# A two-block sequence model on one core: output products of eight finished tiles set between the steps of the last scan

## The reference, cut to what matters

```python
branches = [(ya, a_z), (yb, b_z), (yc, c_z), (yd, d_z), (ym, m_z)]
mixed = jnp.concatenate([y.astype(x.dtype) * jax.nn.silu(z) for y, z in branches], axis=-1)
return x + mixed @ w_out
```

```python
def step(state, inp):
    r_t, w_t, k_t, v_t, kk_t, a_t = inp
    sa = jnp.einsum("bhvk,bhk->bhv", state, -kk_t)
    state = (state * w_t[:, :, None, :] + sa[..., None] * (kk_t * a_t)[:, :, None, :]
             + v_t[..., None] * k_t[:, :, None, :])
    return state, jnp.einsum("bhvk,bhk->bhv", state, r_t)
...
y = rms_norm(y.swapaxes(0, 1), ln_g.reshape(GROUP_HEADS, HEAD_DIM))
y = y + jnp.sum(rh * kh * r_k, axis=-1, keepdims=True) * vh
```

## Time and profile before

| what | us |
|---|---|
| median of three runs | 1772.87 |
| the profiled execution | 1763.42 |
| its span, first to last instruction | 1761.7 |
| pairs, 1565 to 1592 | 27.0 |
| doubling, 1592 to 1643.4 | 51.4 |
| `WT`, `MTt` v and `U`, to 1655.87 | 12.5 |
| scan with all outputs, 1655.87 to 1695.20 | 39.3 |
| output products under the y chain, to 1708.07 | 12.9 |
| turning, gating and splitting y, to 1711.44 | 3.4 |
| the other output products, to 1758.50 | 47.1 |
| last add and store | 3.2 |

### The profile page before, as it was taken

How to read it: one execution, slowest core, us unless ns; L and a number is a source line. 1 busy time by engine, 2 the same in 40 slices (tenths; PEclk the granted TensorE clock), 3 DMA queues, 4 the chain that set the end, 5 groups by cost and what they waited for, 6 DMA issues and landing times. The chain is left out here.

```text
span 1761.7 us, 23121 instructions
## 1 busy us (share of the span) xinstructions
PE 1608.7 (91%) x9729; PEld 1341.3 (76%) x9729; DVE 720.7 (41%) x1479; ACT 519.5 (29%) x841; POOL 593.6 (34%) x247
## 2 busy tenths in 40 slices
PE   6998999999989988989897998999999877959899
PEld 6896876999979765866675997897887643649889
DVE  4031430331163635977665125312301555586331
ACT  2443224331123123243343112342221235211211
POOL 5333420433333263534642333332442360500213
PEclk8999999999999988999998999999999786578869
DMA  4313220225223220320111422242222000000102
GB/s 147 90 57 94 72 72 1 75 94 179 96 72 97 77 79 24 96 72 24 49 48 32 173 73 84 96 128 78 91 95 72 1 0 1 0 30 1 64 26 98
DMA packets 116721, 121.58 MB, mean 69 GB/s; under 512 B 14607, under 2 KB 110841, under 8 KB 116362
## 3 DMA queue, kind: packets, MB, share of 16 engines
q1 hardware_dynamic: 113072, 114.16, 20.6%
q10 hardware_dynamic: 3546, 5.94, 0.9%
HBM read 113.80 MB, written 6.29 MB: 68 GB/s over the span
## 5 line engine op out<-in xcount | busy, mean ns | idle before, releaser
L175 POOL TENSOR_TENSOR w_low<-w_ring,w_high 128x2048 fp32r<-128x2048 f32 (+2 forms) x95 | 422.5, 4448 | 896.9 <-ACT w_high L166 896.8
L191 PE MATMUL ps<-w_high,xT_high 128*128 128x256 f32 (+1 forms) x1056 | 305.9, 290 | 9.9 <-issue 6.9
L191 PE MATMUL ps<-w_high,xT_low 128*128 128x256 f32 (+1 forms) x1056 | 300.9, 285 | 0.0
L191 PE MATMUL ps<-w_low,xT_high 128*128 128x256 f32 (+1 forms) x1056 | 300.9, 285 | 0.0
L166 ACT ACTIVATE w_high<-w_ring 128x2048 fp32r<-128x2048 f32 (+2 forms) x95 | 174.1, 1833 | 362.4 <-PE ps L191 349.7
L191 PE MATMUL ps<-xT_high,w_high 128*128 128x512 f32 (+3 forms) x624 | 255.4, 409 | 8.7 <-DVE mix_a L724 7.7
L191 PE MATMUL ps<-xT_low,w_high 128*128 128x512 f32 (+3 forms) x624 | 250.8, 402 | 0.0
L191 PE MATMUL ps<-xT_high,w_low 128*128 128x512 f32 (+3 forms) x624 | 249.4, 400 | 0.0
L191 PEld LDWEIGHTS ps<-w_high,xT_high 128*128 128x128 f32 x1056 | 204.8, 194 | 15.2 <-issue 14.9
L191 PEld LDWEIGHTS ps<-w_low,xT_high 128*128 128x128 f32 x1056 | 204.8, 194 | 1.3 <-issue 1.2
L191 PEld LDWEIGHTS ps<-w_high,xT_low 128*128 128x128 f32 x1056 | 204.2, 193 | 0.0
(11 more groups left out here) (500 smaller groups left out, 2416.3 us busy)
## 6 DMA issues: line engine op xcount, KB each, us to landing
w_ring<-in_gla_w_in_dram SPq DMA_DIRECT2D x24, 1024.0 KB, 5.4
w_ring<-in_dsa_w_in_dram SPq DMA_DIRECT2D x19, 1024.0 KB, 5.2
w_ring<-in_w_in_dram SPq DMA_DIRECT2D x18, 1024.0 KB, 5.1
w_ring<-in_gla_w_out_dram SPq DMA_DIRECT2D x8, 1024.0 KB, 5.2
w_ring<-in_ple_gate_w_dram SPq DMA_DIRECT2D x8, 1024.0 KB, 5.0
w_ring<-in_dsa_w_out_dram SPq DMA_DIRECT2D x8, 1024.0 KB, 5.0
w_ring<-in_w_out_dram SPq DMA_DIRECT2D x8, 640.0 KB, 4.3
x_scratch<-x SPq DMA_DIRECT2D x4, 1024.0 KB, 6.9
```

The lines of the kernel that those rows point to most:

```text
L175: self.nc.gpsimd.tensor_tensor(self.w_low[:, i % RING, 0:k, 0:cols], self.w_ring[:, n % RING, 0:k, 0:cols], self.w_high[:, i % RING, 0:k, ...
L191: return self.nc.tensor.matmul(out, lhs, rhs, start=first, stop=last, skip_group_check=not check)
```

## The change

- `w_out` is cut the other way: four chunks of 256 columns by the eight finished tiles, and a fifth of 1024 columns by the two own tiles. `slot` lets a ring slot hold the fifth chunk's shape. Each chunk is loaded by one or two DMAs.
- The products of the finished tiles are 16 **units** (`early_out`), one for a chunk and a token tile, 24 split products of 256 columns each, in two banks of PSUM that take turns. VectorE adds each unit to `x_back` (`early_added`). Units 0 to 7 stand in the eight steps of the scan, between the k products and the wait for `sa`; 8 and 9 behind the scan; 10 to 15 behind the last outputs.
- The outputs stand behind the S products instead of ahead of them, two for a step from the second on; the last two behind unit 9. Their four heads share a bank now, and the scaling of y reads them without a permutation.
- The own tiles' products are eight groups (4 token tiles by 2 halves of 512 columns) of 6 split products, at the very end.
- ScalarE makes the first chunk's high half and the high halves of the finished tiles at the start of the block. GpSimd makes that chunk's low half at once, then waits for the four `TiT_init`, then makes `mix_low`.
- To free memory for that, `RKT` gets its own tensor, `Cm` takes the place of `bt`, and `Ti` and `TiT` take the slots of the second chunk.
- The bonus products are made ahead of the scan; VectorE waits for `x_back` there; SP loads a third chunk before `x_back`.

On TensorE, one step of the scan before (the third): `WT` with the state, then k with v (`rwkv_tok`), then two outputs, each with `RKT` (here a part of `branch_room`), `RBT` and the state, then S (`sa,rwkv_tok`).

The diff, cut to its core (`add_sources`, `add_rows` and the removed `project` are told above):

```diff
-        g.add_chunks(t["w_out_2"][0], 0, D, most=MIX_TILES // 2 * P)
+        for a in range(0, D, CHUNK):
+            g.add_rows(t["w_out_2"][0], [(0, OWN_TILES[0]), (OWN_TILES[-1] + 1, MIX_TILES)], a, a + CHUNK)
+        g.add_rows(t["w_out_2"][0], [(OWN_TILES[0], OWN_TILES[-1] + 1)], 0, D)
...
+        RKT = new("RKT", [P, NT, GH, P])
...
-        Ti, RKT = rooms[first_slot], rooms[1 - first_slot]
-        Cm, TiT = rooms[2 + first_slot][:, 0:2], rooms[3 - first_slot]
+        Ti, TiT = rooms[1 - first_slot], rooms[3 - first_slot]
+        Cm = bt[:].rearrange("p a (h t) -> p a h t", h=GH)
+        bonus_v = MTt[:].rearrange("p j h t -> p (j h t)")[:, 0:NT * GW].rearrange("p (j d) -> p j d", j=NT)
...
+                def early_out(u):
+
+                    c, j = early_units[u]
+                    if j == 0:
+                        chunk[0] = g.chunk(pe, w_out + c)
+                    if u == 0:
+                        pe.wait_ge(sem["mix_low"], past["mix_low"] + len(early))
+                    if u < 2:
+                        pe.wait_ge(sem["U_copied"], past["U_copied"] + NT)
+                    else:
+                        pe.wait_ge(sem["early_added"], past["early_added"] + u - 1)
+                    for i, k in enumerate(early_tiles):
+                        ins = g.split_product(ps[:, early_bank(u), 0:CHUNK], columns(s.mix_parts, k, slice(j * P, (j + 1) * P)), columns(chunk[0], i),
+                                              i == 0, i == len(early_tiles) - 1)
+                    ins.then_inc(sem["early_ready"], add("early_ready", 1))
+                    if j == NT - 1:
+                        g.release("early_ready")
...
-
-                    for n in range(2 * (c - 2), 2 * (c - 1)):
-                        if n >= 0:
-                            output(*outputs[n])
-                    pe.wait_ge(sem["sa_ready"], past["sa_ready"] + 2 * c + 2)
+                    early_out(first_early[c])
+                    pe.wait_ge(sem["sa_ready"], past["sa_ready"] + c + 1)
                     for cols, out in place:
                         ins = g.product(out, tok[toks, 0, j, cols], sa[toks, j, cols], False, True, check=False)
                     ins.then_inc(sem["S_ready"], add("S_ready", 1))
-                for n in range(2 * (NCH - 2), len(outputs)):
+                    for n in range(2 * (c - 1), 2 * c):
+                        if n >= 0:
+                            output(*outputs[n])
+                early_out(NCH)
+                early_out(NCH + 1)
+                pe.wait_ge(sem["early_added"], past["early_added"] + NCH + 1)
+                for n in range(2 * (NCH - 1), len(outputs)):
                     output(*outputs[n])
...
+                for u in range(NCH + 2, len(early_units)):
+                    early_out(u)
                 pe.wait_ge(sem["y_final"], past["y_final"] + NT)
                 to_gated(g, pe, y, [4, 5])
+                w = g.chunk(pe, w_out + D // CHUNK)
+                pe.wait_ge(sem["state_new"], past["state_new"] + PAIRS * NCH)
+                pe.wait_ge(sem["early_added"], past["early_added"] + len(early_units))
+                pe.wait_ge(sem["y_gated"], past["y_gated"] + len(OWN))
                 pe.wait_ge(sem["own_low"], past["own_low"] + len(OWN))
-                project(0, 1, OWN, True)
-                for n in range(1, D // CHUNK):
-                    for c in range(2):
-                        project(n, c, halves[c], True)
+                for u, (n, j) in enumerate(own_units):
+                    for i, k in enumerate(OWN):
+                        ins = g.split_product(ps[:, own_bank(u), :], columns(s.mix_parts, k, slice(j * P, (j + 1) * P)), columns(w, i, slice(n * COLS, (n + 1) * COLS)),
+                                              i == 0, i == len(OWN) - 1)
+                    ins.then_inc(sem["own_ready"], add("own_ready", 1))
+                g.release("own_ready")
...
             def _(act):
+                g.split_high(act, w_out + 1)
+                for tiles in early:
+                    nc.scalar.activation(s.mix_parts[0][:, tiles, :], s.mixT[:, tiles, :], ACT.Copy).then_inc(sem["mix_high"], add("mix_high", 1))
...
-                for j in range(NT):
+                g.split_high(act, w_out + 3)
+
+                def y_squares(j):
                     act.wait_ge(sem["y_ready"], past["y_ready"] + j - j % 2 + 2)
-                    sq = RBT[:, j, 0:2, :].rearrange("p h t -> p (h t)").rearrange("p (i b d) -> p b i d", b=2, d=HD)
-                    nc.scalar.activation(sq, y_in(j), ACT.Square).then_inc(sem["y_sq"], add("y_sq", 1))
+                    nc.scalar.activation(RBT[:, j, 0:2, :].rearrange("p h t -> p (h t)"), y_in(j), ACT.Square).then_inc(sem["y_sq"], add("y_sq", 1))
+
+                y_squares(0)
+                y_squares(1)
+                g.split_high(act, w_out + 4)
+                y_squares(2)
+                y_squares(3)
                 act.wait_ge(sem["y_mean_sq"], past["y_mean_sq"] + 1)
                 nc.scalar.activation(ss[:], ss[:], ACT.Sqrt).then_inc(sem["y_root"], add("y_root", 1))
-                g.split_high(act, w_out + 2)
+                g.split_high(act, len(g.chunks))
...
             def _(pool):
-                pool.wait_ge(sem["X_ready"], past["X_ready"] + doubled)
                 g.split_low(pool, w_out + 1)
+                pool.wait_ge(sem["TiT_init"], past["TiT_init"] + NT)
                 for i, tiles in enumerate(early):
                     pool.wait_ge(sem["mix_high"], past["mix_high"] + i + 1)
                     nc.gpsimd.tensor_tensor(s.mix_parts[1][:, tiles, :], s.mixT[:, tiles, :], s.mix_parts[0][:, tiles, :].bitcast(F32), ALU.subtract).then_inc(sem["mix_low"], add("mix_low", 1))
...
+                dve.wait_ge(sem["x_back"], past["x_back"] + 16)
+
+                def early_added(u):
+
+                    c, j = early_units[u]
+                    cols = slice(c * CHUNK, (c + 1) * CHUNK)
+                    dve.wait_ge(sem["early_ready"], past["early_ready"] + u + 1)
+                    nc.vector.tensor_tensor(x_back[:, j, cols], x_back[:, j, cols], ps[:, early_bank(u), 0:CHUNK], ALU.add).then_inc(sem["early_added"], add("early_added", 1))
...
+                    early_added(first_early[c])
...
             def _(sp):
+                g.load_chunks(sp, w_out + RING + 1)
                 sp.wait_ge(sem["YT_ready"], past["YT_ready"] + doubled)
                 sp.dma_start(x_back, g.x_dram).then_inc(sem["x_back"], add("x_back", 16))
                 g.load_chunks(sp)
```

117 lines of the change are left out of this document (63 added, 54 removed).

## The result

The changed kernel takes 1758.62 us (median of 8 runs, 1749.62 to 1762.14) beside 1771.28 for the kernel before on the same chip (8 runs, 1763.38 to 1775.2): a ratio of 0.9928, 95% interval 0.9901 to 0.9955. That is 12.7 us where 15.5 were forecast, 2.8 too many. The time itself is 1.6 us above the 1757 of the forecast and inside its range of 1749 to 1769; the two misses differ mainly because the kernel before has a median of 1771.28 in eight runs and had 1772.87 in three. The two profiled executions differ by 12.6 us: 1750.8 us (span 1749.1) against 1763.4 (span 1761.7).

A forecast was written before the change was run, and what follows sets the result against it. TensorE's instruction stream was taken as the bound, half of it slow because the scan alone does not keep the clock up. Terms -16.0 - 2.6 - 1.4 + 2.4 + 2.1 = -15.5 gave 1772.9 - 15.5 = 1757 us, range 1749 to 1769.

The forecast's parts named there:

- The bound and the mechanism: TensorE's instruction stream bounds, half of it slow; dense units between the scan's steps hold its clock at 2.4 GHz.
- the first rival: Scan: the clock falls in every step, so units start or stay at 1.2 GHz; 1780 to 1793 us, chance 8%.
- rival of the clock: Scan: clock falling in every step, 1780 to 1793 us, 8%; or now and then, 1760 to 1775, 14%.
- The scan's products and gaps: Scan: small products at the upper clock save 16.0 us; units and moved outputs cover TensorE's waits for VectorE, -4.0.
- the ratio of 0.49: Scan: an output's first two records, 0.24 us apiece at 1.2 GHz, against 0.118 for that form just before the scan.
- Changes between small and full tiles: Scan: switching between small and dense products twice a step, 16 times, halved at the upper clock, costs 1.4 us.
- The slow start: Output products behind the scan: 15 products at 0.213 us instead of 0.118 go away, -1.4 us.
- The pause: Behind the scan: 3.37 us for transposes, gating and splitting the own tiles, and one slow stretch after it, stay: 0.
- First place: Block's start: GpSimd's low half of the first chunk holds VectorE's `LT` times `levelT` product, +2.4 us (0 to 4.65).
- Second place: Doubling's start: GpSimd's `mix_low` ops take turns with VectorE's `Cm` masks and TensorE waits, +2.1 us (0 to 9.2).
- the shift: The doubling was to be shifted by 4 to 5 us at its start, no more at its end.
- The sum: Whole kernel: -16.0 - 2.6 - 1.4 + 2.4 + 2.1 = -15.5 us, to 1757.

## Why the prediction was right, and where it was off

**The bound and the mechanism** were right: the clock of the scan went from 0.52 to 1.00, the units lasted 3.02 us (2.8 forecast, 5.1 by the first rival), TensorE stood 0.58 us in the scan, and the scan lasted 42.0 us (1661.15 to 1703.17), as forecast. No rival of the clock came true in the profiled execution; the experiments show that the dense work is the cause.

**The scan's products and gaps** were forecast at -16.0 and -4.0; the small work of the scan with its waits went from 39.33 to 21.3 us (68.45 from 1661.15 to 1729.60, less 47.1 of unit products), **-18.0**. The gaps were right, 4.58 to 0.58. The products gave 14.0: 34.75 us became about 20.8. The step that was off is the ratio of 0.49. It set the first two records of an output, 0.48 us among other products, against an unbroken run of 32 of the same form, 0.118 each. Rows of the kernel before (WT and k products to the first output; `sa` products to the next output), then of the changed one (WT and k products to the unit; `sa` and WT stand above; two outputs of the last step):

```profile
1670.33 0.58 PE L191 MATMUL ps<-rwkv_state,WT 64*64 64x64 f32 x5 [0.57 <-DVE rwkv_state L2837]
...
1671.38 0.69 PE L191 MATMUL ps<-rwkv_tok,branch_room 128*128 128x64 f32 x2
...
1688.82 0.64 PE L191 MATMUL ps<-sa,rwkv_tok 64*64 64x64 f32 x8
1689.38 0.69 PE L191 MATMUL ps<-rwkv_tok,branch_room 128*128 128x64 f32 x2
```
```profile
1665.77 0.27 PE L209 MATMUL ps<-rwkv_state,WT 64*64 64x64 f32 x2 [0.58 <-DVE rwkv_state L2896]
...
1666.38 0.39 PE L209 MATMUL ps<-w_high,mix_high 128*128 128x256 f32 x1
...
1703.17 0.43 PE L209 MATMUL ps<-rwkv_tok,RKT 128*128 128x64 f32 x2
1703.44 0.39 PE L209 MATMUL ps<-sa,RBT 128*128 128x64 f32 x2
...
1704.02 0.43 PE L209 MATMUL ps<-rwkv_tok,RKT 128*128 128x64 f32 x2
```

In the scan itself the same two records go from 0.48 to 0.27 us (0.56), an output from 1.45 to 0.85 (0.59), the WT and k products behind a wait from 1.05 to 0.61 (0.58), a step's `sa` products from 0.56 to 0.38 (0.68). All of it together, less the 1.3 us that were fast already, comes to 19.5 / 33.4 = 0.58, and that is the 2 us. The kernel before showed it in the scan's first step, before the clock fell: its WT and k products took 0.65 us there.

**Changes between small and full tiles**, +1.4: the 384 products took 47.1 us, **+1.8** over 384 x 0.118. **The slow start**, -1.4: before, the first 96 products took 13.03 us (1695.20 to 1708.23), **-1.7**. **The pause** stayed, 3.29 for 3.37, and so did a slow stretch behind it: 47.03 us for 45.3 of products before, 12.98 for 11.2 after. That last part was no certainty, since half of the kernels with the pause ran these products in 11.35. From the scan's start to the end 87.95 instead of 105.83, -17.9, where -20.0 was forecast.

**First place**, +2.4: the op's own stretch was right (2.82 us, near 3 forecast, +2.14). What was mis-sized is the term: "VectorE is busy for 22.84 of that stage's 27 us, so the delay stays" takes it that nothing else comes. TensorE's wait of 4.69 us behind the product, and its lower clock in the tiles that follow, added 1.7: **+3.9** by the profiles (2.6 to 3.9 over seven kernels).

**Second place**, +2.1: **+1.8** by the two profiles (67.31 for 65.55), 2.5 to 2.9 by taking it out. The course was as forecast: the first mask goes through, GpSimd's op of 3.45 us goes next, the second mask ends at about 1597.6 and TensorE's second product starts at 1597.68, 3.8 us behind the first. The Trainium skill, SBUF — State Buffer, section "SBUF: two separate sides", gives the shared pair to whoever starts first; read to the letter the second mask could have had it, with a term of 0. The trace decides for turns: three masks of 0.69 us alone take 8.37, each of the last two behind one of GpSimd's ops, though VectorE had them queued without a gap. The forecast that the shift would be 4 to 5 us at the doubling's start was a little off: 3.5 there, and 5.3 from its second unit on to the scan.

**The sum**: -17.9 + 3.9 + 1.8 = -12.2, and the block began 0.36 us earlier, which makes the 12.6 between the profiles. Against -15.5 that is 3.3 short: 2.1 in the scan to the end, 1.1 at the two meetings.

## What to carry to other kernels

When small products are repriced at the other clock, take the ratio from the same sequence of products at both clocks, not from a run of one form alone. A transfer of work to GpSimd is priced where it lies: the same op cost 2.6 to 3.9 us against VectorE's critical products and 0.3 to 1.8 where VectorE mostly reads PSUM; where VectorE works two units ahead, ops of about 3.5 us cost TensorE nothing and one of 4.7 us cost it a wait of 0.96. And look at what a delay sets off: here 2.14 us on VectorE stopped TensorE for 4.69, it came back at the lower clock, and the stage lost 3.9.

## What was not expected of the hardware

- TensorE busy for 98.7% of 46 us with 64x64 and 128x64 products stood at a granted clock of 0.53; with 4 wide products of 256 columns per step of 3.2 us, at 1.00 in the profiled execution.
- In a mixed sequence the upper clock, twice the lower one, does not halve the small products: eight 64x64 ones ahead of an output go from 0.56 to 0.38 us, an output from 1.45 to 0.85. In an unbroken run at the upper clock the 128x64 form takes 0.118 apiece.
- GpSimd's three ops took 10.43 us while VectorE took turns with them, and 9.16 where VectorE did not ask.
